# Hybrid HGRN2 / RWKV-7 layer with a routed mixture of experts: products with the state made for two chunks in one round, with three state buffers in place of two and one

## The reference

```python
    def step(S, blk):
        qc, kc, vc, gc = blk
        b = jnp.cumsum(gc, axis=2)
        ...
        o = (jnp.einsum('bhts,bhsv->bhtv', scores, vc)
             + jnp.einsum('bhtd,bhdv->bhtv', qc * jnp.exp(b), S))
        ...
        S_new = (jnp.exp(b_last[:, :, 0, :])[..., None] * S
                 + jnp.einsum('bhsd,bhsv->bhdv', kc * jnp.exp(b_last - b), vc))
        return S_new, o
```

```python
        sa = jnp.einsum('bhij,bhj->bhi', S, -kk_t)
        S = (S * jnp.exp(lw_t)[:, :, None, :]
             + sa[..., None] * (kk_t * a_t)[:, :, None, :]
             + v_t[..., None] * k_t[:, :, None, :])
        y = jnp.einsum('bhij,bhj->bhi', S, r_t)
```

## Time and profile before

| what | value |
|---|---|
| median of 3 timed runs | 3090.16 us (3088.65 to 3098.03) |
| span of the profiled execution, first to last instruction | 3087.1 us |
| PE busy in the span | 2833.2 us (92%) |
| DVE, ACT, POOL busy | 1408.9, 857.0, 330.0 us (46%, 28%, 11%) |
| 16 iterations of the recurrence, first to last h_update | 1158.4 to 1689.9 us |

### The profile page before, as it was taken

The page is one execution under the profiler, slowest core; times in us unless marked ns, Lnnn a source line. Parts: engine busy times, 40 slices in busy tenths (PEclk is TensorE's granted clock), DMA queues, the critical chain, the costliest instruction groups (busy, mean ns, idle before and its releaser), DMA issues. The chain is left out here.

```text
span 3087.1 us, 86581 instructions
## 1 busy us (share of the span) xinstructions
PE 2833.2 (92%) x36669; PEld 1696.2 (55%) x36670; DVE 1408.9 (46%) x3464; ACT 857.0 (28%) x1845; POOL 330.0 (11%) x567
## 2 busy tenths in 40 slices
PE   5998999999999839999989699976999999999988
PEld 2432445454454538888888545543555555555543
DVE  2246365655655636666666534453222222222218
ACT  2447343433343413333333212120000000000005
POOL 0000000000000000000000100002222222222224
PEclk8999999999999969999999799987999999999999
DMA  7541123223242285555554395672798668778758
GB/s 277 215 146 41 69 92 128 92 98 121 86 136 83 100 233 139 161 156 140 140 146 145 110 331 201 227 265 67 280 362 304 217 234 303 285 272 306 269 208 343
DMA packets 368368, 580.97 MB, mean 188 GB/s; under 512 B 38590, under 2 KB 231670, under 8 KB 365080
## 3 DMA queue, kind: packets, MB, share of 16 engines
q1 hardware_dynamic: 312888, 483.56, 45.4%
q0 software_dynamic: 18832, 70.53, 6.5%
q10 hardware_dynamic: 36432, 23.70, 2.7%
HBM read 412.09 MB, written 165.60 MB: 187 GB/s over the span
## 5 line engine op out<-in xcount | busy, mean ns | idle before, releaser
L451 PE MATMUL pj_P<-pj_hT,pj_wc 128*128 128x448 f32 (+2 forms) x1600 | 590.4, 516 | 0.9 <-ACT pj_stage L579 0.9
L2590 PE MATMUL moe_PG<-wgu,moe_xT 128*32 128x256 f32 x9600 | 551.6, 382 | 0.0
L451 PEld LDWEIGHTS pj_P<-pj_hT,pj_wc 128*128 128x128 f32 x1600 | 294.1, 189 | 256.5 <-issue 239.4
L2590 PEld LDWEIGHTS moe_PG<-wgu,moe_xT 128*32 128x32 f32 x9600 | 297.4, 110 | 207.2 <-issue 27.8
L2420 DVE TENSOR_TENSOR moe_sg<-moe_sg,moe_PG 128x128 f32<-128x128 f32 x150 | 43.2, 288 | 556.8 <-ACT moe_sg L2469 556.8
L2601 PE MATMUL moe_PTY<-wd,moe_hT 128*32 128x256 f32 x4800 | 286.5, 379 | 0.6 <-DVE moe_hT L2425 0.6
L2469 ACT ACTIVATE moe_sg<-moe_PG 128x128 f32<-128x128 f32 x150 | 41.7, 278 | 794.2 <-PE moe_PG L2590 794.2
L2008 PE MATMUL merge_PO<-merge_w,merge_mT 128*128 128x512 f32 x544 | 238.9, 597 | 0.4 <-DVE merge_x L2122 0.4
L2601 PEld LDWEIGHTS moe_PTY<-wd,moe_hT 128*32 128x32 f32 x4800 | 155.9, 110 | 103.5 <-DVE moe_y L2413 0.8
L2008 PEld LDWEIGHTS merge_PO<-merge_w,merge_mT 128*128 128x128 f32 x544 | 102.5, 191 | 123.8 <-issue 123.2
L2512 POOL DMA_INDIRECT moe_xg<-scratch_h,moe_row x154 | 149.0, 967 | 125.8 <-POOL moe_xc L2525 109.3
(11 more groups left out here) (403 smaller groups left out, 4206.4 us busy)
## 6 DMA issues: line engine op xcount, KB each, us to landing
wgu<-in_w_gate SPq DMA_DIRECT2D x32, 2048.0 KB, 9.7
wgu<-in_w_up SPq DMA_DIRECT2D x32, 2048.0 KB
wd<-in_w_down SPq DMA_DIRECT2D x32, 2048.0 KB
re_hkf<-scratch_hk SPq DMA_DIRECT2D x60, 640.0 KB, 7.9
scratch_y_rows<-merge_zeros SPq DMA_DIRECT2D x51, 512.0 KB, 4.7
re_rkf<-scratch_rk SPq DMA_DIRECT2D x68, 320.0 KB, 6.0
scratch_hk<-pj_hk SPq DMA_DIRECT2D x16, 1344.0 KB, 5.8
scratch_y_rows<-moe_y ACTq DMA_DIRECT2D x604, 32.0 KB
```

The costliest lines, as they stand in the source:

```text
L451: ins = eng.matmul(bank[:, 0:wp], wc[:, j, k, :], hT[:, k, k0:k0 + wp], start=(k == 0), stop=(k == KD - 1), skip_group_check=True)
L2590: ins = eng.matmul(PG[32 * q:32 * q + 32, 0, 0:256].rearrange("p (a b) -> p a b", a=2), x_rows, wgu[p][:, :, k, 128 * q:128 * q + 128], st ...
```

## The change

The products of both chunks with their states are made in one round each. `h_inter(b, 0)` and `h_inter(b, 1)` become one `h_inter(b)` of 8 matmuls at the place where `h_inter(b, 1)` stood, alternating between the chunks. `y_from_state(b, 0)` and `y_from_state(b, 1)` become one `y_from_state(b)` of 16 matmuls at the second one's place, four matmuls in turn going to the four quarters of the array. `from_state` keeps its two calls. So that both chunks' states are there at once, S and ST have three buffers each, taken in turn by `state(b, c)`. The update of ST no longer waits for the products of its own block, and that of S no longer for the first chunk's `h_inter`. The room comes from `STd`, the state of the running sequences, which now lies in a buffer of `rkf` that the last loop iteration has read. The number of matmuls is the same.

```diff
-        S = sb("S", [128, 2, 4, 128])
-        ST = sb("ST", [128, 4, RW_N])
+        S = sb("S", [128, 3, 4, 128])
+        ST = sb("ST", [128, 3, 4, RW_N])
...
-        STd = sb("STd", [128, NSEQ // 2, 4, 2, RW_N])
+        STd = rkf[(TAIL - 1) % 3].rearrange("p c s w -> p (c s w)")[:, 0:NSEQ // 2 * 8 * RW_N].rearrange("p (q m s v) -> p q m s v", q=NSEQ // 2, m=4, s=2)
...
+        def state(b, c):
+
+            return (2 * b + c) % 3
...
-            def h_inter(b, c):
+            def h_inter(b):
 
                 p = b % 2
-                if c == 0:
-                    if b:
-                        eng.wait_ge(ev("o_scaled"), b)
-                        eng.wait_ge(ev("s_kept"), 2 * b)
-                    else:
-                        eng.wait_ge(ev("zeroed"), 1)
-                else:
-                    eng.wait_ge(ev("s_kept"), 2 * b + 1)
+                if b:
+                    eng.wait_ge(ev("o_scaled"), b)
+                eng.wait_ge(ev("s_kept"), 2 * b + 1)
                 eng.wait_ge(ev("qb_kept"), b + 1)
                 for h in range(4):
-                    o = slice(128 * h, 128 * h + 128)
-                    ins = eng.matmul(out_o(chunk(c), h), qbb[p][:, h, chunk(c)], S[:, c, h, :], start=(h == 0), stop=False, skip_group_check=True)
+                    for c in range(2):
+                        ins = eng.matmul(out_o(chunk(c), h), qbb[p][:, h, chunk(c)], S[:, state(b, c), h, :], start=(h == 0), stop=False, skip_group_check=True)
...
-            def y_from_state(b, c):
+            def y_from_state(b):
...
+                eng.wait_ge(ev("st_kept"), 2 * b + 1)
+                for m in range(4):
+                    for c in range(2):
+                        for h in (2 * m, 2 * m + 1):
+                            ins = eng.matmul(out_y(chunk(c), h), rkf[b % 3][half(h), m, RK_A1, chunk(c)], ST[half(h), state(b, c), m, :],
+                                             start=False, stop=False, skip_group_check=True)
...
                 if back:
                     h_update(b)
-                    h_inter(b, 0)
                     from_state(b, 0)
...
                     to_state(b, 0)
-                    y_from_state(b, 0)
...
                 if back:
-                    h_inter(b, 1)
+                    h_inter(b)
                     h_intra(b)
...
                     to_state(b, 1)
-                    y_from_state(b, 1)
+                    y_from_state(b)
...
-                    eng.wait_ge(ev("inter_made"), 2 * b + 1)
                     eng.wait_ge(ev("s_kept"), 2 * b + 1)
...
-                eng.wait_ge(ev("ys_made"), 2 * b + c + 1)
-                eng.tensor_tensor(ST[:, :, :], sum_[:, :, :], ends[:, 0, :, 2 * b + c:2 * b + c + 1].to_broadcast([128, 4, RW_N]), ALU.mult).then_inc(ev("st_kept"), 1)
+                if c == 0 and b:
+                    eng.wait_ge(ev("ys_made"), b)
+                eng.tensor_tensor(ST[:, state(b, c + 1), :, :], sum_[:, :, :], ends[:, 0, :, 2 * b + c:2 * b + c + 1].to_broadcast([128, 4, RW_N]), ALU.mult).then_inc(ev("st_kept"), 1)
```

More of the change, by code:

```diff
@@ L1068, in _ @@
             eng.wait_ge(ev("s_kept"), 2 * PT)
-            eng.dma_start(t["new_hgrn_p"][0, 0].rearrange("h k v -> k h v"), S[:, 0, :, :]).then_inc(ev("s_out"), 16)
+            eng.dma_start(t["new_hgrn_p"][0, 0].rearrange("h k v -> k h v"), S[:, state(PT, 0), :, :]).then_inc(ev("s_out"), 16)
             eng.wait_ge(ev("sout_kept"), 1)
@@ L1127, in from_state @@
             def from_state(b, c):
-                p = b % 2
                 if b or c:
                     eng.wait_ge(ev("st_kept"), 2 * b + c)
+                else:
+                    eng.wait_ge(ev("zeroed"), 1)
                 eng.wait_ge(ev("tokens_made"), b + 1)
                 for h in range(8):
-                    ins = eng.matmul(out_g(chunk(c), h), rkf[b % 3][half(h), h // 2, RK_A0, chunk(c)], ST[half(h), h // 2, :],
+                    ins = eng.matmul(out_g(chunk(c), h), rkf[b % 3][half(h), h // 2, RK_A0, chunk(c)], ST[half(h), state(b, c), h // 2, :],
                                      start=False, stop=(h == 7), skip_group_check=True)
                 ins.then_inc(ev("as_made"), 1)
-            def y_from_state(b, c):
[L1140 to L1143, removed]
+            def y_from_state(b):
[5 more added lines that the diff above has]
+                                             start=False, stop=False, skip_group_check=True)
                 ins.then_inc(ev("ys_made"), 1)
@@ L1180, in y_out @@
                 p = b % 2
-                eng.wait_ge(ev("ys_made"), 2 * b + 2)
+                eng.wait_ge(ev("ys_made"), b + 1)
                 for h in range(8):
@@ L1406, in _ @@
             for m in range(4):
-                ins = eng.transpose(P_C[0:RW_N, 128 * m:128 * m + 128], ST[:, m, :], ident)
+                ins = eng.transpose(P_C[0:RW_N, 128 * m:128 * m + 128], ST[:, state(PT, 0), m, :], ident)
             ins.then_inc(ev("st_turned"), 1)
@@ L1454, in _ @@
             ins.then_inc(ev("ys_made"), 1)
-            eng.wait_ge(ev("ys_made"), 2 * TAIL + 1)
+            eng.wait_ge(ev("ys_made"), TAIL + 1)
             for h in range(8):
@@ L1602, in _ @@
                 if f >= 2:
-                    eng.wait_ge(ev("inter_made"), 2 * (f - 1))
+                    eng.wait_ge(ev("inter_made"), f - 1)
                 eng.tensor_copy(qbb[p][:, :, :], hkf[p][:, :, HK_B, :]).then_inc(ev("qb_kept"), 1)
@@ L1637, in _ @@
             step(eng.memset(S[:, 0, :, :], 0.0))
-            step(eng.memset(ST[:, :, :], 0.0))
+            step(eng.memset(ST[:, 0, :, :], 0.0))
             settle()
@@ L1654, in update_s @@
                     if b:
-                        eng.wait_ge(ev("inter_made"), 2 * b)
+                        eng.wait_ge(ev("inter_made"), b)
                 else:
-                    eng.wait_ge(ev("inter_made"), 2 * b + 1)
                     eng.wait_ge(ev("s_kept"), 2 * b + 1)
                 for h in range(4):
-                    ins = eng.scalar_tensor_tensor(S[:, 1 - c, h, :], S[:, c, h, :], ends[:, 1, h, 2 * b + c:2 * b + c + 1],
+                    ins = eng.scalar_tensor_tensor(S[:, state(b, c + 1), h, :], S[:, state(b, c), h, :], ends[:, 1, h, 2 * b + c:2 * b + c + 1],
                                                    (P_D, P_C)[c][:, 128 * h:128 * h + 128], ALU.mult, ALU.add)
@@ L1666, in update_st @@
                 eng.wait_ge(ev("st_made"), 2 * b + c + 1)
-                step(eng.tensor_tensor(sum_[:, :, :], ST[:, :, :], heads(P_ST[:, 0:256], 4), ALU.add))
+                step(eng.tensor_tensor(sum_[:, :, :], ST[:, state(b, c), :, :], heads(P_ST[:, 0:256], 4), ALU.add))
                 settle()
-                eng.wait_ge(ev("ys_made"), 2 * b + c + 1)
-                eng.tensor_tensor(ST[:, :, :], sum_[:, :, :], ends[:, 0, :, 2 * b + c:2 * b + c + 1].to_broadcast([128, 4, RW_N]), ALU.mult).then_inc(ev("st_kept"), 1)
+                if c == 0 and b:
+                    eng.wait_ge(ev("ys_made"), b)
+                eng.tensor_tensor(ST[:, state(b, c + 1), :, :], sum_[:, :, :], ends[:, 0, :, 2 * b + c:2 * b + c + 1].to_broadcast([128, 4, RW_N]), ALU.mult).then_inc(ev("st_kept"), 1)
                 eng.wait_ge(ev("st_kept"), 2 * b + c + 1)
```

## The result

The changed kernel takes 3101.15 us (median of 19 runs, 3095.60 to 3105.67), the kernel before 3094.59 us in the same sessions (19 runs); the ratio is 1.0021, with a 95% interval of 1.0014 to 1.0029. It is 6.6 us slower, which is the price of rival (b), not of my forecast.

What follows compares the result with a forecast made beforehand. DVE bounds each iteration's beginning, then ACT's copies and instruction blocks hold PE: -23.8 + 16.3 (wait for DVE) + 1.3 (ACT's copy) + 6.2 (instructions) = 0, so median 3090 us; forecast 3086 to 3093, range 3078 to 3100.

Steps and rivals of the forecast that it cites:

- rival (b): At instruction-block borders: blocks come later by their request, 16 x 0.40 = 6.4 us slower, 3096.4; chance 0.14.
- The beginning belongs to DVE: Up to the third turn: PE waits for DVE's updates of S, so 16.3 of the 23.8 us are gone.
- The rounds side by side: h_inter's 16 records, alternating column halves, take 1.02 us again; y_from_state's 32, in quarters, 0.46 us as 16 did.
- The blocks of instructions: Borders between turns and first_y: later blocks use up PE's 0.39 us; between -0.39 and +0.40 us, taken as 0.
- Rival (a): At the borders: the instructions hide, PE keeps its 0.39 us, 6.2 us in all, 3083.9; chance 0.19.
- rival (d): At the third turn: PE's 1.3 us standstill lowers the clock, 27 us slower in all 16 blocks, 3117; chance 0.08.
- (c): Iteration's beginning: S's updates can start earlier, DVE doesn't hold it, the whole 23.8 us gained, 3066.4; chance 0.07.
- (e): Third turn and borders: wait for DVE shrinks in part, instructions hide in part, some 13 us gained, 3077; chance 0.05.

Runs made afterwards that it cites:

- the first three groups of experiments: Each part of the change alone (1.0017, 1.0000); changed kernel with h_inter ahead of the third turn (1.0002); three with DVE's updates of S earlier (1.0032, 1.0023, 1.0020).
- the HGRN2 part alone: Only h_inter of both chunks in one round and three buffers for S, y_from_state and ST as before, against the kernel before: 1.0017.
- the other part: Only y_from_state of both chunks in one round and three buffers for ST, h_inter and S as before, against the kernel before: 1.0000.

## Why the prediction was wrong

**The beginning belongs to DVE: held.** The updates of S start 3.44 us after keep_xtf (1483.46 - 1480.02), as predicted (3.45). PE's weight load waits 1.23 us at the third turn; 1.30 was predicted, and the 0.07 between them are DVE's updates, 2.27 us where they took 2.34. The sum is 16.5 us on PEld, not 20: there are 15 such waits in the stretch, and in a few of them PE came late from a stop ahead of it.

**The rounds side by side: held.** h_inter's 16 records span 1.09 us (about 1.1 predicted). It starts 0.50 us earlier after h_update, for 0.39 predicted; the 0.07 of the updates are part of the difference. y_from_state's 32 records span 0.85 us where no stop lies among them (about 0.7 predicted), as its 16 did, and from first_y to make_y it is 3.78 us in both kernels without the transfers: the grown round costs nothing.

**The blocks of instructions: here it failed.** "I take 0, the value by which the end of the traffic sets the arrival." I had both ends, -0.39 and +0.40 us a block of frames, and chose between them by a stretch that ended with the traffic. The change measures +6.6 us over 16 blocks, 0.41 each, at the upper end and within 0.2 us of rival (b)'s sum. So the step that failed is this term, put at 0 with the end of the traffic as its reason. That the borders took what PE won is shown: up to make_y the same gain (0.46 and 0.47 us) is there when the transfers are left out and when they are moved behind the stretch, the loss of 6.6 us is gone in both pairs, and no kernel that only made PE earlier was faster. That anything of the gain is left in the time of the whole kernel, neither pair shows by itself. Rival (a), the instructions hide, holds only there.

Why it is a loss and not merely no gain can be seen in part, since the trace holds the packets of the queue "instruction" one by one. Counting 128 matmul records from border to border, one packet starts between any border and the next in the recurrence of both kernels, and every stop for instructions of over 0.25 us ends 1.2 to 1.7 us after a packet's end. So the prediction was right that a block comes only when the one before it has begun. What varies is how long the packet takes to start: behind such stops 1.2 us (median, in both kernels) with the DMA engines nearly idle, 2.6 us before and 2.4 after with them busy.

In three of the 15 iterations, the second, fifth and last, a border lies at or just behind the place that h_inter(b, 0) had. PE passes it 1.6, 1.4 and 2.0 us after h_update's start in the changed kernel, 0.5 to 0.8 us earlier than in the kernel before, and yet the next packet starts later, at 7.2, 8.6 and 7.4 us, where it started at 5.0, 4.8 and 5.5. PE stops for 1.17, 2.98 and 0.65 us there; before, it did not stop. The fifth iteration of the changed kernel starts at 1300.08; its stop, and the queue's row from 1308.6 to 1309.9 (from 1301.5 to 1308.6 it has none):

```profile
1311.28 0.69 PE L1201 MATMUL re_P<-re_rkf 64*64 64x128 f32 x4 [2.98 <-issue]
```

```profile
q8 instruction: 1, 0.02, 5.8%
```

This is no accident of one profile: the changed kernel and the five of the first three groups of experiments that have no h_inter(b, 0) there start these packets at 6.5 to 8.6 us, the two kernels that keep it at 4.8 to 5.5. The kernel with the HGRN2 part alone has the three stops, 5.0 us in all, beside a loss of 5.3 us by its ratio; the kernel with the other part has none of them and no loss. Rival (b) had its request go out later; these borders are passed earlier, so that its sum was met within 0.2 us is luck.

Three things stay open. At other borders stops shrink as well as grow (one of 2.81 us before is 1.20 after), so the three are not the whole account. The kernel with h_inter in the wait has them too (4.9 us) and yet no loss (1.0002), so it wins about as much elsewhere; with DVE's updates moved as well the loss is there again (1.0020). And why the packet behind an earlier border starts later in those microseconds, in which the hk tiles are on their way, no run here shows.

Part of the loss is the clock: in the recurrence of the changed kernel 17.1 us were at half clock (6.8, 3.4 and 6.8, from 1310.0, 1463.6 and 1610.4 us), 10.2 before, which at the prediction's price (1.7 us for 3.4) is worth an estimated 3.4 of the 8.6 us between the two profiled executions. These places lie at stops for instructions, of 2.98 (the one above), 1.66 and 3.80 us; none lies behind one of the 15 waits for DVE, of up to 1.0 us, alone, and without transfers the waits stay and the clock is 1.00. So rival (d)'s mechanism is there, at another stop than it named. But with fewer transfers outstanding, one profile each, half clock took 0, 23.9 and 23.9 us of the recurrence in the three kernels, and I can't say whether waits for DVE add to what stops begin. How the 6.6 us divide between the three stops, the other borders and the clock stays open.

**The level.** 4.4 us of the distance to 3090 are in the three runs of the kernel before, not in the change: 3090.16 + 6.6 would have lain in the range.

**The other rivals.** (c) and (e) needed DVE or the instructions to give way, and neither did. The Trainium skill (Runtime: NRT & Kernel Launch, Instruction fetch mechanics) calls a border mostly hidden. The runs bound that: up to make_y with the DMA engines idle (share 0.01) nothing of it shows; with the transfers there, an iteration has 2.1 us of stops before and 3.1 us after (30.8 and 46.0 us by 15); with the transfers in the levels, 4.9 (72.9 by 15).

None of the kernels that do the whole work beats the kernel before. What is to be had at most stands in the pair without transfers, 31 us, most of it stops for instructions; how to have it with the transfers there, no run shows.

## What to carry to other kernels

Before counting what an engine saves, look at what its instructions cost to bring: cut the stretch at its "issue" stops, compare the time of a block's work with the time that a block takes to come, with the DMA engines as busy as they are there. Where the two were about equal here, work taken off that engine was no gain, and input transfers cost less where a block of instructions lasts long than where it is short. If the trace holds the instruction queue's packets, read when each starts: here an earlier border could get its block later. When both ends of an unknown are in hand, ask of every row whether it tells them apart before taking the middle.

## What the runs showed that I had not expected

- Moving the same transfers by 16 us, from long-lasting to short instructions on PE, cost 53 us (1.0164), more than leaving most of them out gained (31 us, 0.9904).
- Giving out one or two transfers at a time in place of four made the kernel no faster (1.0021, 1.0026, 1.0018), though half the packets or fewer were out at a time.
- In the recurrence of the changed kernel the granted clock fell to 0.50 for 3.4 or 6.8 us at three stops for instructions, of 1.7 to 3.8 us, but not at one of 3.3 us (L1309), and stayed at 1.00 behind the 1.0 us waits for DVE where no such stop was near.
